# Moving half of the memory projections of a two-layer block from the opening to the border between the layers

## The chip, the cores and the metric

The kernel runs on one core of one Trainium2 chip. A core has a matrix engine (TensorE, "PE"), a vector engine (DVE), a scalar engine (ACT), GpSimd (POOL) and a queue for transfers on SyncE (SP). Each engine executes its own list of instructions in order; semaphores order them among each other. The metric is the device time of one execution in microseconds (us), lower is better.

## What is computed

Two blocks follow each other on the same 512 x 1024 activations; the change touches the first. It has two layers, and both attend to one memory of 256 rows, with keys and values of their own:

```python
def mem_cross_attention(q_mem, mem_n, w_kv):
    kv = mem_n @ w_kv                     # 256 x 1024 @ 1024 x 1024
    km, vm = split_cols(kv, [MEM_W, MEM_W])
    ...
    s = einsum('bshd,bmhd->bhsm', q, km) / sqrt(HEAD_DIM)
    return einsum('bhsm,bmhd->bshd', softmax(s), vm)

def first_block(x, mem, ...):
    mem_n = rmsnorm(mem, mem_norm_g)
    for i in range(2):
        h = rmsnorm(x, norm_g[i])
        # i == 0: forgetting attention, i == 1: retention
        proj = h @ w_in[i]
        memo = mem_cross_attention(q_mem, mem_n, w_mem_kv[i])
        o = concat([main, memo]) * silu(z)
        x = x + o @ w_out[i]
    return rmsnorm(x, final_norm_g)
```

`mem_n` is the same for both layers, so the keys and values of layer 2 can be made at any time before its memory attention.

## The kernel before

All matrices are float32. Every operand is split into a high half (rounded, `wh`, `HH`, `MH`) and a low half (the rest, `wl`, `HL`, `ML`), and each product is three matmuls: high by high, high by low, low by high. Activations lie transposed: X is 8 tiles of 128 features x 512 tokens, the memory MX is 8 tiles of 128 x 256.

**Weights** arrive in a planned order (`weight_plan`, line 95) as blocks of 512 KB, 128 x 1024. SP loads them into five buffers `raw` (`load_raw`, 278). `split_next` (321) makes a block's halves in one of three buffers: ACT copies raw to `wh`, then POOL subtracts to give `wl`, after which the raw buffer is loaded anew. `take` (342) hands the next block, a **slot**, to the matmuls; when it hands out slot u, it has put the splits up to slot u + 2 on ACT's and POOL's lists, and the split of u + 2 waits until the matmuls of slot u - 1 have released its buffer. Some blocks ("ada", 303) are no slots: DVE multiplies them with a vector, for the second block of the model.

**A unit** is two slots, 1024 x 256 weights: `unit_f` (393, out features x tokens, two banks) and `unit_t` (398, tokens x out features) each have 2 x 24 matmuls, on bank 0 and 1 unless told otherwise. The banks' owner before must have been read out (`bank.free`).

**The opening** (line 495 on). SP issues the loads: parameters, a raw block, the memory in two halves, a raw block, constants, a raw block, X in one piece, raw blocks. ACT and DVE make MH and ML, then the squares of the memory (`add_square`, 433: ACT squares into one of two buffers T, DVE adds up in ACC). A loop of eight units follows, `i` = 0 to 7: four for layer 1 and four for layer 2, two of keys (km) and two of values (vm) each, all on banks 0 and 1. The memory's 1/rms is applied when a unit's result is stored; `mem_rstd` (527) makes it: matmuls with ones sum over features, ACT does Ln, Exp (row form RM), Ln, Exp (column form). It stands between the halves of unit 0. Beside units 1 and 2 X is squared, `acc_rstd` (462) after unit 3 makes R, the 1/rms of X, and beside units 4 to 7 `normed` (467) makes two tiles of HH and HL each: DVE multiplies X by the gain and R into a T buffer, ACT copies to HH, and POOL (two of three tiles) or DVE subtracts to HL and so frees T. Then a single slot gives the forget gate (`slot_128`), tile by tile, and `layer_mem` (695) makes the queries and gates of the memory heads.

**The end of layer 1.** `project_out` (670) has 16 slots in four groups n of four q, all on banks 0 and 1. `steps` at (n, q) are put out right behind that slot's matmuls. After the fourth slot of a group DVE adds the banks to X tiles 2n and 2n+1, which frees the banks, and `add_square` follows each addition:

```python
            for j in range(2):
                t = 2 * n + j
                m = tt(X[:, t, :], X[:, t, :], bank[j].ap, ALU.add, ...)
                bank[j].free = [m]
                ... add_square(X[:, t, :], ...)
```

**The border.** After it `next_h` (849) makes R and all eight tiles of HH and HL, and `layer_mem(1, ...)` begins with a unit that needs them.

Of the kernel before, what the change touches and what calls it, by code (L numbers as in the profile page):

```python
# [8 lines left out]
ALU = mybir.AluOpType  # L9
ACT = mybir.ActivationFunctionType  # L10
# [84 lines left out]
def weight_plan():  # L95

    plan = []

    def pair(w, k0, k1, cols):
        for k in range(k0, k1, 4):  # L100
            plan.append(("w", w, k, cols))

    def ada(i):
        plan.append(("ada", i // 8, i % 8, None))

    left = list(range(47, -1, -1))
    for i in range(8):
        pair("kv%d" % (i // 4), 0, 8, (256 * (i % 4),))
    plan.append(("f", "fox", 0, None))
    for cols in [4620, 5132 + 1536, 4876, 5132 + 1792]:  # L110
        pair("fox", 0, 8, (cols,))
        ada(left.pop())
        ada(left.pop())
    for p in range(6):
        for cols in (1536 + 256 * p, 256 * p, 3072 + 256 * p, 5132 + 256 * p):
            pair("fox", 0, 8, (cols,))
            ada(left.pop())
            if p < 2:
                ada(left.pop())
    for n in range(4):  # L120
        for k in (12, 0, 4, 8):
            pair("out0", k, k + 4, (256 * n,))
            if left:
                ada(left.pop())
    for cols in [3072, 3584 + 1536, 3328, 3584 + 1792]:
        pair("ret", 0, 8, (cols,))
    for p in range(6):
        for cols in ((128 * p, 768 + 128 * p), (1536 + 256 * p,), (3584 + 256 * p,)):
            pair("ret", 0, 8, cols)
    for n in range(4):  # L130
        for k in (12, 0, 4, 8):
            pair("out1", k, k + 4, (256 * n,))
    for cols in (512, 1024, 768, 1280, 0, 256, 2560, 1536):
        pair("in2", 0, 8, (cols,))
    plan.append(("g", "in2", 0, None))
    for cols in (1792, 2048, 2304, 2816):
        pair("in2", 0, 8, (cols,))
    for n in range(4):
        pair("out2", 0, 8, (256 * n,))

    def up(g):
        for n in range(4):
# [19 lines left out]
def build(nc, a, out, stack):  # L162
# [10 lines left out]

    pe, dve, act, pool, sp = (Line(count("s_" + n)) for n in ("pe", "dve", "act", "pool", "sp"))
    s_raw = [count("s_raw%d" % i) for i in range(NRAW)]
    s_x, s_par = count("s_x"), count("s_par")
    s_mem = [count("s_mem%d" % i) for i in range(2)]
    s_sw = [count("s_sw%d" % i) for i in range(2)]
    s_d = [count("s_d%d" % i) for i in range(2)]
# [141 lines left out]
    def split_next():  # L321
        i = st["split"]
        if i >= len(plan):
            return False
        st["split"] += 1
        s, m = i % NRAW, landed[i]
        kind = plan[i][0]
        if kind == "ada":
            ada(plan[i][1], plan[i][2], s, m)
            load_raw()  # L330
            return split_next()
        u = st["nsplit"]
        st["nsplit"] += 1
        q = u % NW
        m1 = copy(wh[:, q, :], raw[:, s, :], after=[m, *w_free[q]])
        m2 = pool.do(G.tensor_tensor, wl[:, q, :], raw[:, s, :], wh[:, q, :].bitcast(F32), ALU.subtract, after=[m1])
        raw_free[s] = [m2]
        ready[u] = m2
        load_raw()
        return True  # L340
# [126 lines left out]
    def normed(src, g, rm, n, xh, xl, after, bias=None, ks=range(8), before=None, scale=None):  # L467
# [21 lines left out]
        if low:  # L489
# [2 lines left out]
        return ms  # L492


    MX = at("MX", [128, 8, 256], 148)
    MH, ML = at("MH", [128, 8, 256], 124, F32R), at("ML", [128, 8, 256], 132, F32R)
    maskf = at("maskf", [128, 128], 183.5)
    RM = at("RM", [128, 256], C0 + 8)
    m_par = sp.dma(SP.dma_start, par[:, :], a["par"], s_par)
    load_raw()  # L500
    m_mem = [sp.dma(SP.dma_start, MX[:, 4 * i:4 * i + 4, :], a["memT"][:, 4 * i:4 * i + 4, :], s_mem[i])
             for i in range(2)]
    load_raw()
    m_cst = sp.dma(SP.dma_start, ident[:, :], a["cst"][:, 0:128], s_c[0])
    m_cst = sp.dma(SP.dma_start, ones[:, :], a["cst"][:, 128:256], s_c[0])
    m_cst = sp.dma(SP.dma_start, maskf[:, :], a["cst"][:, 256:384], s_c[0])
    M["cst"], M["par"] = m_cst, m_par
    load_raw()
    m_x = sp.dma(SP.dma_start, X[:, :, :], a["xT"], s_x)
    for _ in range(NRAW - 3):  # L510
        load_raw()
    m = dve.do(V.memset, eps[:, 0:1], 1e-6)
    M["eps"] = dve.do(V.memset, one, 1.0)
    mem_h = Tiles()
    split_next()
    for k in range(8):
        m = copy_scaled(MH[:, k, :], MX[:, k, :], P("gm", k), [m_mem[k // 4], m_par])
        mem_h.high.append(m)
        mem_h.append(stt(ML[:, k, :], MX[:, k, :], P("gm", k), MH[:, k, :].bitcast(F32), ALU.mult, ALU.subtract,
                         after=[m]))  # L520
        if k == 3:
            split_next()
    for k in range(8):
        add_square(MX[:, k, :], 256, k == 0, [m_mem[k // 4]])
    rcol = small["tq"]

    def mem_rstd():

        e, m = rstd(ACC[:, 0:256], [M["acc"]], 256, 1024, RM[:, :], [], bank[6])
        for t in range(2):  # L530
            e = mm(bank[7].ap[:, t:t + 1], ACC[:, 128 * t:128 * t + 128], ones[:, 0:1], t == 0, t == 1,
                   after=[*bank[7].free], mark=(t == 1))
        m2 = afn(rcol[:, 0:2], bank[7].ap[:, 0:2], ACT.Ln, after=[e], scale=1.0 / 1024, bias=eps[:, 0:1])
        bank[7].free = [m2]
        M["acc free"] = [e]
        return m, afn(rcol[:, 0:2], rcol[:, 0:2], ACT.Exp, after=[m2], scale=-0.5)

    M["kv"], x_h = [], Tiles()
    for i in range(8):
        l, j = i // 4, i % 4  # L540
        if j < 2:
            for kh in range(2):
                features(MH, ML, range(4 * kh, 4 * kh + 4), 256, kh == 0, kh == 1, mem_h, bank[0:2])
                if i + kh == 0:
                    m_rm, m_rc = mem_rstd()
            e0 = tt(km[l][:, 2 * j, :], bank[0].ap[:, 0:256], RM[:, :], ALU.mult, after=[bank[0].done, m_rm])
            e1 = tt(km[l][:, 2 * j + 1, :], bank[1].ap[:, 0:256], RM[:, :], ALU.mult, after=[bank[1].done])
            bank[0].free, bank[1].free = [e0], [e1]
        else:
            unit_t(MH, ML, 2, mem_h)  # L550
            for t in range(2):
                e1 = copy_scaled(vm[l][:, t, 256 * (j - 2):256 * (j - 2) + 256], bank[0].ap[:, 256 * t:256 * t + 256],
                                 rcol[:, t:t + 1], [bank[0].done, m_rc])
            bank[0].free = [e1]
        M["kv"].append(e1)
        if i == 0:
            vcopy(identb[:, :], ident[:, :], after=[m_cst])
            M["bf"] = vcopy(maskb[:, :], maskf[:, :])
            for n, d in (("c", small["sc"]), ("cc", small["scc"])):
                m = afn(d[:, :], P(n, 0, 8), ACT.Tanh, after=[m_par], scale=0.5)  # L560
                m = ts(d[:, :], d[:, :], 1.0, 0.5, ALU.add, ALU.mult, after=[m])
                silu_c.append(tt(d[:, :], d[:, :], P(n, 0, 8), ALU.mult, after=[m, m_par]))
        if i in (1, 2):
            for k in range(4 * i - 4, 4 * i):
                add_square(X[:, k, :], T, k == 0, [m_x])
        if i == 3:
            rm = acc_rstd(T)
        if 3 < i:
            ks = range(2 * i - 8, 2 * i - 6)
            part = normed(X, lambda k: P("g0", k), rm, T, HH, HL, [m_par], ks=ks)  # L570
            x_h += part
            x_h.high += part.high
# [97 lines left out]
    def project_out(l, steps):  # L670

        for n in range(4):
# [146 lines left out]
    for p in range(6):  # L819
# [904 lines left out]
```

How the kernel before makes its waits and increments, by code:

```python
    def replay(self, eng):  # L72
        for w in self.work:
            if w[0] is None:
                eng.wait_ge(w[1], w[2])
            else:
                i = w[0](*w[1], **w[2])
                if w[3] is not None:
                    i.then_inc(w[3], w[4])
```

## Time and profile before

| | us |
|---|---|
| three runs, median (lowest to highest) | 1754.67 (1751.62 to 1755.99) |
| the profiled execution, first to last instruction | 1755.0 |
| PE busy | 1668.5 (95%) |
| DVE, ACT, POOL busy | 779.3, 670.3, 712.4 |
| chain that ended last: PE, DVE, ACT, POOL | 81%, 10%, 4%, 2% |
| POOL wl, 246 times | 2497 ns each |
| ACT wh, 246 times | 1054 ns each |

The rows of the next section come from a profile of one execution. A timeline row is: start (us), duration (us), engine, line, operation, what it writes and reads, count. Where an engine sat idle before it, the brackets give for how long and what ended that. PEclk is the granted clock of PE as a share of 2.4 GHz.

### The profile page before, as it was taken

How to read it: one execution, taken by the hardware profiler on the slowest of the kernel's cores; microseconds unless marked ns; L12 is line 12 of the kernel's file. 1: busy time of each engine (PE TensorE's matmuls, PEld its weight loads, DVE VectorE, ACT ScalarE, POOL GpSimd, SP SyncE). 2: the span in 40 equal slices, each digit the busy share in tenths (PEclk: the TensorE clock that was granted, in tenths of full speed). 3: DMA queues.
4: the chain of work that ended last, by engine and by line, in shares of the span. 5: the costliest groups of instructions: out<-in, count | busy, mean ns of one | idle time of the engine just before them, and what ended most of it. 6: DMA issues, size and time to landing. Idle time of an engine off the chain costs nothing.

```text
span 1755.0 us, 19876 instructions
## 1 busy us (share of the span) xinstructions
PE 1668.5 (95%) x8208; PEld 1364.0 (78%) x8208; DVE 779.3 (44%) x1083; ACT 670.3 (38%) x966; POOL 712.4 (41%) x333
## 2 busy tenths in 40 slices
PE   5898999999999899999999999989989899999997
PEld 5776888888878677888887767778977688888885
DVE  5588775564653333443432646563262421111113
ACT  6543333333322342444444453225633443232322
POOL 4744334433334343333333324342412265454542
PEclk9999999999999999999999999999999999999999
DMA  6434343324244223223323222112201133222221
GB/s 228 133 114 159 136 147 136 138 97 150 89 144 151 72 73 114 82 92 102 96 91 112 73 108 72 48 72 75 73 1 36 61 112 100 99 100 96 96 84 48
DMA packets 51953, 175.98 MB, mean 100 GB/s; under 512 B 6284, under 2 KB 6924, under 8 KB 51352
## 3 DMA queue, kind: packets, MB, share of 16 engines
q1 hardware_dynamic: 51864, 174.73, 28.9%
q8 instruction: 64, 1.05, 0.2%
q14 instruction: 25, 0.20, 0.0%
HBM read 169.44 MB, written 2.12 MB: 98 GB/s over the span
## 4 chain that ended last, share of the span: by engine, by line
PE 81%; DVE 10%; ACT 4%; POOL 2%; issue 2%; DMA 1%; SPq 0%; DVEq 0%; ACTq 0%; POOLq 0%
PE banks L77 81%; DVE T L77 2%; DVE ada L77 2%; ACT L77 1%; DVE TM L77 1%; POOL wl L77 1%; DVE Sc L77 1%; DVE X L77 1%; ACT R L77 1%; DVE ACC L77 0%; ACT Sc L77 0%; ACT wh L77 0%; DVE HL L77 0%; DVE Y L77 0%; DMA raw<-wst_dram 0%
## 5 line engine op out<-in xcount | busy, mean ns | idle before, releaser
L77 POOL TENSOR_TENSOR wl<-raw,wh 128x1024 fp32r<-128x1024 f32 x246 | 612.3, 2497 | 674.4 <-ACT wh L77 674.4
L77 PE MATMUL banks<-HH,wh 128*128 128x512 f32 x1040 | 416.9, 401 | 13.9 <-ACT HH L77 9.1
L77 PE MATMUL banks<-HL,wh 128*128 128x512 f32 x1040 | 408.0, 392 | 1.0 <-DVE HL L77 0.4
L77 PE MATMUL banks<-HH,wl 128*128 128x512 f32 x1040 | 407.2, 392 | 0.0
L77 ACT ACTIVATE wh<-raw 128x1024 fp32r<-128x1024 f32 x246 | 257.6, 1054 | 380.6 <-PE banks L77 354.5
L77 PEld LDWEIGHTS banks<-HH,wh 128*128 128x128 f32 x1040 | 196.9, 189 | 61.6 <-issue 15.5
L77 PEld LDWEIGHTS banks<-HL,wh 128*128 128x128 f32 x1040 | 196.1, 189 | 46.1 <-DVE HL L77 3.1
L77 PEld LDWEIGHTS banks<-HH,wl 128*128 128x128 f32 x1040 | 197.0, 189 | 42.0 <-issue 2.6
L77 PE MATMUL banks<-wh,HH 128*128 128x256 f32 x448 | 128.7, 287 | 2.0 <-ACT QX L77 2.0
L77 PE MATMUL banks<-wh,HL 128*128 128x256 f32 x448 | 127.4, 284 | 0.0
L77 PE MATMUL banks<-wl,HH 128*128 128x256 f32 x448 | 127.4, 284 | 0.0
L77 PE MATMUL banks<-OH,wh 128*128 128x512 f32 x256 | 104.4, 408 | 3.0 <-DVE X L77 2.2
L77 DVE SCALAR_TENSOR_TENSOR X<-banks,mod,X 128x512 f32<-128x512 f32 x40 | 30.0, 751 | 163.3 <-PE banks L77 163.3
L77 PE MATMUL banks<-OL,wh 128*128 128x512 f32 x256 | 100.0, 391 | 0.0
L77 PE MATMUL banks<-OH,wl 128*128 128x512 f32 x256 | 100.0, 391 | 0.0
L77 PE MATMUL banks<-FHI,wh 128*128 128x512 f32 x256 | 99.6, 389 | 0.0
L77 PE MATMUL banks<-FHI,wl 128*128 128x512 f32 x256 | 99.6, 389 | 0.0
L77 PE MATMUL banks<-FLO,wh 128*128 128x512 f32 x256 | 99.6, 389 | 0.0
L77 POOL TENSOR_TENSOR OL<-T,OH 128x512 fp32r<-128x512 f32 x22 | 29.2, 1328 | 171.0 <-ACT OH L77 171.0
L77 ACT ACTIVATE T<-banks 128x512 f32<-128x512 f32 x78 | 46.5, 596 | 122.3 <-PE banks L77 121.3
L77 PEld LDWEIGHTS banks<-wh,HH 128*128 128x128 f32 x448 | 86.6, 193 | 3.6 <-issue 2.8
L77 ACT ACT_TABLE_LOAD x69 | 88.5, 1283 | 2.0 <-PEq L1715 0.7
(285 smaller groups left out, 2578.1 us busy)
## 6 DMA issues: line engine op xcount, KB each, us to landing
raw<-wst_dram SPq DMA_DIRECT2D x294, 512.0 KB, 3.3
CB<-sums_dram SPq DMA_DIRECT2D x12, 256.0 KB, 3.0
D<-dec_dram SPq DMA_DIRECT2D x12, 256.0 KB, 2.6
X<-xT_dram SPq DMA_DIRECT2D x1, 2048.0 KB, 10.7
out_dram<-X SPq DMA_DIRECT2D x8, 256.0 KB
QS<-QX SPq DMA_DIRECT2D x24, 64.0 KB, 2.6
KSw<-KX SPq DMA_DIRECT2D x24, 64.0 KB, 2.0
MX<-memT_dram SPq DMA_DIRECT2D x2, 512.0 KB, 6.0
```

The source lines that it names most:

```text
L77: i = w[0](*w[1], **w[2])
```

## The change

- The plan has four pairs of kv blocks in the opening and four, for layer 2, behind `out0`.
- In the opening the memory's squares come ahead of the first unit, into ACC2. Units rotate over the bank pairs (0, 1), (2, 3), (4, 5), (0, 1). `mem_rstd` is put out after unit 1, R of X after unit 2, and HH and HL are made in two groups of four tiles around unit 3. X comes in two loads. Slot 0's low half is made by DVE.
- In `project_out(0)` the memory is loaded again (into HH's place), split into MH and ML and squared in two steps, and its 1/rms is made at (2, 3).
- At the border unit 0 of layer 2 runs first, then R of X is put out, then HH and HL in groups of 2, 3 and 3 tiles with a unit behind each.

```diff
-    for i in range(8):
-        pair("kv%d" % (i // 4), 0, 8, (256 * (i % 4),))
+    for i in range(4):
+        pair("kv0", 0, 8, (256 * i,))
...
+    for i in range(4):
+        pair("kv1", 0, 8, (256 * i,))
     for cols in [3072, 3584 + 1536, 3328, 3584 + 1792]:
         pair("ret", 0, 8, (cols,))
...
-        m2 = pool.do(G.tensor_tensor, wl[:, q, :], raw[:, s, :], wh[:, q, :].bitcast(F32), ALU.subtract, after=[m1])
+        if u == 0:
+            m2 = tt(wl[:, q, :], raw[:, s, :], wh[:, q, :].bitcast(F32), ALU.subtract, after=[m1])
+        else:
+            m2 = pool.do(G.tensor_tensor, wl[:, q, :], raw[:, s, :], wh[:, q, :].bitcast(F32), ALU.subtract, after=[m1])
...
+    def load_mem(l, after=()):
+        memory[l]["at"] = [sp.dma(SP.dma_start, memory[l]["MX"][:, 4 * i:4 * i + 4, :], a["memT"][:, 4 * i:4 * i + 4, :],
+                                  s_mem[i], after=after) for i in range(2)]
+
+    def mem_half(l, k, after=()):
+
+        d = memory[l]
+        h = d.setdefault("h", Tiles())
+        m = copy_scaled(d["MH"][:, k, :], d["MX"][:, k, :], P("gm", k), [d["at"][k // 4], m_par, *after])
+        h.high.append(m)
+        h.append(stt(d["ML"][:, k, :], d["MX"][:, k, :], P("gm", k), d["MH"][:, k, :].bitcast(F32), ALU.mult, ALU.subtract,
+                     after=[m]))
...
+    def mem_rstd(l):
+
+        d = memory[l]
+        last = M.pop("last", None)
+        e, m = rstd(ACC2[:, 0:256], [M["acc2"]], 256, 1024, d["RM"][:, :], [M["v read"]] if l else [], bank[6])
+        for t in range(2):
+            e = mm(bank[7].ap[:, t:t + 1], ACC2[:, 128 * t:128 * t + 128], ones[:, 0:1], t == 0, t == 1,
+                   after=[*bank[7].free], mark=(t == 1))
+        m2 = afn(rcol[:, 0:2], bank[7].ap[:, 0:2], ACT.Ln, after=[e], scale=1.0 / 1024, bias=eps[:, 0:1])
...
+    pairs = [bank[0:2], bank[2:4], bank[4:6], bank[0:2]]
...
+    mem_squares(0, range(8))
+    kv_matmuls(0, 0, pairs[0])
+    x_squares(range(0, 3))
+    kv_matmuls(0, 1, pairs[1])
+    mem_rstd(0)
+    for j in range(2):
+        kv_store(0, j, pairs[j])
+    vcopy(identb[:, :], ident[:, :], after=[m_cst])
+    M["bf"] = vcopy(maskb[:, :], maskf[:, :])
+    x_squares(range(3, 8))
+    kv_matmuls(0, 2, pairs[2])
+    rm = acc_rstd(T)
+    kv_store(0, 2, pairs[2])
+    for ks in (range(0, 4), range(4, 8)):
+        part = normed(X, lambda k: P("g0", k), rm, T, HH, HL, [m_par], ks=ks)
+        x_h += part
+        x_h.high += part.high
+        if ks[0] == 0:
+            kv_matmuls(0, 3, pairs[3])
+    kv_store(0, 3, pairs[3])
...
-    project_out(0, {(0, 0): [lambda: fox_turn(11)], (0, 1): [lambda: fox_attend(11)]})
+    h_read = M["v read"]
+
+    def mem_again(ks):
+        for k in ks:
+            mem_half(1, k, [M["v read"], M["z read"], M["pt read"]])
+        mem_squares(1, ks)
+
+    project_out(0, {(0, 0): [lambda: load_mem(1, [h_read]), lambda: fox_turn(11)], (0, 1): [lambda: fox_attend(11)],
+                    (1, 0): [lambda: mem_again(range(0, 4))], (2, 0): [lambda: mem_again(range(4, 8))],
+                    (2, 3): [lambda: mem_rstd(1)]})
...
-    M["pe"] = bank[1].done
-    hs = next_h(lambda k: P("g1", k))
+    out0_done = bank[1].done
+
+    pairs = [bank[2:4], bank[4:6], bank[0:2], bank[2:4]]
+    hs = Tiles()
+    kv_matmuls(1, 0, pairs[0])
+    rm = acc_rstd(T)
+    kv_store(1, 0, pairs[0])
+    for j, ks in ((1, range(0, 2)), (2, range(2, 5)), (3, range(5, 8))):
+        part = normed(X, lambda k: P("g1", k), rm, T, HH, HL, [M["x", 7], out0_done, memory[1]["h"][-1]], ks=ks)
+        hs += part
+        hs.high += part.high
+        kv_matmuls(1, j, pairs[j])
+        kv_store(1, j, pairs[j])
+    M["pe"] = pairs[3][0].done
```

`kv_matmuls` is the unit's matmuls as before, `kv_store` the multiplication by 1/rms into km (DVE) or vm (ACT), `mem_squares` the squares of MX.

## Rows read from the trace of the kernel before

**Rows 1.** The page's table of engines: busy us, share of the span, instructions.
```profile
PE 1668.5 (95%) x8208; PEld 1364.0 (78%) x8208; DVE 779.3 (44%) x1083; ACT 670.3 (38%) x966; POOL 712.4 (41%) x333
```

**Rows 2.** Timeline of PE in the opening: matmuls with idle time before them.
```profile
8.66 0.58 PE L77 MATMUL banks<-MH,wh 128*128 128x256 f32 x1 [8.66 <-POOL wl L77]
...
18.74 1.22 PE L77 MATMUL banks<-ACC,ones 128*128 128x256 f32 x2 [5.14 <-DVE ACC L77]
...
71.47 0.58 PE L77 MATMUL banks<-wh,MH 128*128 128x256 f32 x1 [2.53 <-POOL wl L77]
...
81.22 0.47 PE L77 MATMUL banks<-HH,wh 128*128 128x512 f32 x1 [1.02 <-ACT vm L77]
...
88.50 0.50 PE L77 MATMUL banks<-HH,wh 128*128 128x512 f32 x1 [1.56 <-DVE R L77]
```

**Rows 3.** Windows: length, PE, PEld, DVE, ACT, POOL busy (instructions), PEclk, DMA, GB/s.
```profile
20.50:23.00 2.50, 2.50 (x13) 2.50 (x14) 0.00 (x0) 2.45 (x4) 0.97 (x1) 0.50 0.21 57
62.90:68.90 6.00, 5.97 (x48) 5.81 (x48) 4.80 (x3) 3.17 (x4) 6.00 (x4) 1.00 0.55 175
70.90:77.60 6.70, 6.13 (x28) 6.13 (x29) 6.67 (x4) 2.12 (x3) 6.70 (x4) 0.50 0.48 159
602.30:606.70 4.40, 4.12 (x8) 2.21 (x8) 3.06 (x3) 1.79 (x3) 2.50 (x2) 0.50 0.00 0
```

**Rows 4.** Timeline of PE in the projection's beginning and at the border.
```profile
507.72 0.69 PE L77 MATMUL banks<-ident,Sc 128*128 128x128 f32 x2 [3.01 <-DVE Sc L77]
...
602.31 0.76 PE L77 MATMUL banks<-HH,wh 128*128 128x512 f32 x1 [4.36 <-ACT HH L77]
...
617.70 0.59 PE L77 MATMUL banks<-km,Qt 128*128 128x256 f32 x2
```

**Rows 5.** Timeline of POOL in the opening: low halves of slots 0 and 2.
```profile
6.26 2.34 POOL L77 TENSOR_TENSOR wl<-raw,wh 128x1024 fp32r<-128x1024 f32 x1 [5.82 <-ACT wh L77]
...
19.11 2.36 POOL L77 TENSOR_TENSOR wl<-raw,wh 128x1024 fp32r<-128x1024 f32 x1 [5.80 <-ACT wh L77]
```

**Rows 6.** Timelines of POOL and DVE: tile normalisation beside wl, and alone.
```profile
53.08 5.19 POOL L77 TENSOR_TENSOR wl<-raw,wh 128x1024 fp32r<-128x1024 f32 x2 [3.32 <-ACT wh L77]
...
54.61 4.20 DVE L77 SCALAR_TENSOR_TENSOR T<-X,par,R 128x512 f32<-128x512 f32 x2
...
600.75 1.41 DVE L77 SCALAR_TENSOR_TENSOR T<-X,par,R 128x512 f32<-128x512 f32 x2 [4.64 <-ACT R L77]
```

**Rows 7.** Timeline of ACT: the chains of the memory's and of X's 1/rms.
```profile
19.05 1.28 ACT L77 ACT_TABLE_LOAD   x1
20.34 0.47 ACT L77 ACTIVATE RM<-banks,eps 128x256 f32<-128x256 f32 x1
...
25.44 0.20 ACT L77 ACTIVATE tq<-tq 128x2 f32<-128x2 f32 x1
...
48.12 1.28 ACT L77 ACT_TABLE_LOAD   x1
...
51.42 0.63 ACT L77 ACTIVATE R<-R 128x512 f32<-128x512 f32 x1
```

**Rows 8.** Timelines of DVE and ACT around the end of slot (2, 3).
```profile
570.94 0.69 DVE L77 TENSOR_TENSOR X<-X,banks 128x512 f32<-128x512 f32 x1
...
573.66 0.69 DVE L77 TENSOR_TENSOR X<-X,banks 128x512 f32<-128x512 f32 x1 [0.64 <-PE banks L77]
...
571.66 0.64 ACT L77 ACTIVATE T<-X 128x512 f32<-128x512 f32 x1 [3.21 <-DVE X L77]
```

**Rows 9.** Timeline of POOL: the last low half at the border.
```profile
613.28 1.29 POOL L77 TENSOR_TENSOR HL<-T,HH 128x512 fp32r<-128x512 f32 x1 [1.96 <-DVE HL L77]
```

**Rows 10.** The page's list of DMA issues: KB each, us to landing.
```profile
X<-xT_dram SPq DMA_DIRECT2D x1, 2048.0 KB, 10.7
```

**Rows 11.** Timeline of ACT in the output projection: one slot's high half.
```profile
545.62 1.06 ACT L77 ACTIVATE wh<-raw 128x1024 fp32r<-128x1024 f32 x1 [4.38 <-PE banks L77]
```

**Rows 12.** Groups by form, 0 to 100 us: busy, mean ns, idle before.
```profile
L77 DVE SCALAR_TENSOR_TENSOR T<-X,par,R 128x512 f32<-128x512 f32 x8 | 17.5, 2227 | 1.2 <-POOL HL L77 1.2
```

More of the change, by code:

```diff
@@ L175, in build @@
     s_raw = [count("s_raw%d" % i) for i in range(NRAW)]
-    s_x, s_par = count("s_x"), count("s_par")
+    s_x, s_par = [count("s_x%d" % i) for i in range(2)], count("s_par")
     s_mem = [count("s_mem%d" % i) for i in range(2)]
@@ L492, in normed @@
         return ms
-    MX = at("MX", [128, 8, 256], 148)
-    MH, ML = at("MH", [128, 8, 256], 124, F32R), at("ML", [128, 8, 256], 132, F32R)
     maskf = at("maskf", [128, 128], 183.5)
-    RM = at("RM", [128, 256], C0 + 8)
+    rcol = small["tq"]
+    memory = [dict(MX=at("MX0", [128, 8, 256], 148), MH=at("MH0", [128, 8, 256], 124, F32R),
+                   ML=at("ML0", [128, 8, 256], 132, F32R), RM=at("RM0", [128, 256], C0 + 8)),
+              dict(MX=at("MX1", [128, 8, 256], 60), MH=at("MH1", [128, 8, 256], C0, F32R),
+                   ML=at("ML1", [128, 8, 256], C0 + 8, F32R), RM=at("RM1", [128, 256], C0 + 16))]
@@ new lines, in mem_squares @@
+    def mem_squares(l, ks):
+        for k in ks:
+            add_square(memory[l]["MX"][:, k, :], 256, k == 0, [memory[l]["at"][k // 4]], ACC2, name="acc2")
+    def mem_rstd(l):
[6 more added lines that the diff above has]
+        m2 = afn(rcol[:, 0:2], bank[7].ap[:, 0:2], ACT.Ln, after=[e], scale=1.0 / 1024, bias=eps[:, 0:1])
+        bank[7].free = [m2]
+        M["acc2 free"] = [e]
+        d["rm"], d["rc"] = m, afn(rcol[:, 0:2], rcol[:, 0:2], ACT.Exp, after=[m2], scale=-0.5)
+        if last:
+            M["last"] = last
@@ new lines, in kv_matmuls, with kv_store @@
+    def kv_matmuls(l, j, banks):
+        d = memory[l]
+        if j < 2:
+            for kh in range(2):
+                features(d["MH"], d["ML"], range(4 * kh, 4 * kh + 4), 256, kh == 0, kh == 1, d["h"], banks)
+        else:
+            unit_t(d["MH"], d["ML"], 2, d["h"], banks)
+    def kv_store(l, j, banks):
+        d = memory[l]
+        if j < 2:
+            e0 = tt(km[l][:, 2 * j, :], banks[0].ap[:, 0:256], d["RM"][:, :], ALU.mult, after=[banks[0].done, d["rm"]])
+            e1 = tt(km[l][:, 2 * j + 1, :], banks[1].ap[:, 0:256], d["RM"][:, :], ALU.mult, after=[banks[1].done])
+            banks[0].free, banks[1].free = [e0], [e1]
+        else:
+            for t in range(2):
+                e1 = copy_scaled(vm[l][:, t, 256 * (j - 2):256 * (j - 2) + 256], banks[0].ap[:, 256 * t:256 * t + 256],
+                                 rcol[:, t:t + 1], [banks[0].done, d["rc"]])
+            banks[0].free = [e1]
+        M["kv"].append(e1)
@@ L499, in build @@
     m_par = sp.dma(SP.dma_start, par[:, :], a["par"], s_par)
     load_raw()
-    m_mem = [sp.dma(SP.dma_start, MX[:, 4 * i:4 * i + 4, :], a["memT"][:, 4 * i:4 * i + 4, :], s_mem[i])
-             for i in range(2)]
+    load_mem(0)
     load_raw()
@@ L508, in build @@
     load_raw()
-    m_x = sp.dma(SP.dma_start, X[:, :, :], a["xT"], s_x)
+    m_x = [sp.dma(SP.dma_start, X[:, 4 * i:4 * i + 4, :], a["xT"][:, 4 * i:4 * i + 4, :], s_x[i]) for i in range(2)]
     for _ in range(NRAW - 3):
@@ L513, in build @@
     M["eps"] = dve.do(V.memset, one, 1.0)
-    mem_h = Tiles()
     split_next()
     for k in range(8):
[L517 to L520, printed above, removed]
+        mem_half(0, k)
         if k == 3:
             split_next()
-    for k in range(8):
-        add_square(MX[:, k, :], 256, k == 0, [m_mem[k // 4]])
@@ L525, in build @@
[L525 to L536, printed above, removed]
@@ L538, in build @@
-    M["kv"], x_h = [], Tiles()
[L539 to L572, printed above, removed]
@@ new lines, in build, with x_squares @@
+    M["kv"], x_h = [], Tiles()
+    pairs = [bank[0:2], bank[2:4], bank[4:6], bank[0:2]]
+    def x_squares(ks):
+        for k in ks:
+            if k == 7:
+                last_square(X[:, k, :], [m_x[1]])
+            else:
+                add_square(X[:, k, :], T, k == 0, [m_x[k // 4]])
+    mem_squares(0, range(8))
[6 more added lines that the diff above has]
+    vcopy(identb[:, :], ident[:, :], after=[m_cst])
@@ new lines, in build @@
+    M["bf"] = vcopy(maskb[:, :], maskf[:, :])
[10 more added lines that the diff above has]
+    kv_store(0, 3, pairs[3])
+    for n, d in (("c", small["sc"]), ("cc", small["scc"])):
+        m = afn(d[:, :], P(n, 0, 8), ACT.Tanh, after=[m_par], scale=0.5)
+        m = ts(d[:, :], d[:, :], 1.0, 0.5, ALU.add, ALU.mult, after=[m])
+        silu_c.append(tt(d[:, :], d[:, :], P(n, 0, 8), ALU.mult, after=[m, m_par]))
@@ L679, in project_out @@
                 t = 2 * n + j
-                m = tt(X[:, t, :], X[:, t, :], bank[j].ap, ALU.add, after=[bank[j].done, m_x])
+                m = tt(X[:, t, :], X[:, t, :], bank[j].ap, ALU.add, after=[bank[j].done, *m_x])
                 bank[j].free = [m]
@@ L844, in build @@
         fox_scores(2 * p + 1)
-    project_out(0, {(0, 0): [lambda: fox_turn(11)], (0, 1): [lambda: fox_attend(11)]})
-    M["R free"] = [M["v read"], *M["R free"]]
-    def next_h(g, bias=None, extra=()):
-        rm = acc_rstd(T)
-        return normed(X, g, rm, T, HH, HL, [M["x", 7], M["pe"], *extra], bias)
-    M["pe"] = bank[1].done
-    hs = next_h(lambda k: P("g1", k))
+    h_read = M["v read"]
+    def mem_again(ks):
+        for k in ks:
+            mem_half(1, k, [M["v read"], M["z read"], M["pt read"]])
[3 more added lines that the diff above has]
+                    (2, 3): [lambda: mem_rstd(1)]})
+    M["R free"] = [M["v read"], *M["R free"]]
+    out0_done = bank[1].done
[11 more added lines that the diff above has]
+    M["pe"] = pairs[3][0].done
     QA, QB, KR = at("QA", [128, T], C0), at("QB", [128, T], C0 + 2), at("KR", [128, T], C0 + 4)
```

## Prediction

> **What bounds the kernel now.** I read the page's engine table first: TensorE (PE) is busy for 95% of 1755.0 us [rows 1]. The change computes nothing less and nothing more (four units of 48 matmuls move from one place to another), so its worth can only lie in PE's idle time and in time at the lower clock, at the two places it touches. I then read PE's own timeline for the idle time ahead of each matmul, and the other engines' timelines for what ended it.
>
> In the opening PE starts at 8.66 us, when POOL has made the first low half, waits 5.14 us at 18.74 for the squares of the memory, and then loses 1 to 2.5 us at nearly every unit; ahead of the second, third and fourth unit of layer 2 it is a wait for POOL's wl (1.27, 1.41 and 2.53 us; the last is shown). The forget slot starts at 81.22 and the layer's first full unit at 88.50 [rows 2]. One unit of memory keys or values (2 slots, 48 matmuls) is 6.00 us between 62.90 and 68.90 with the granted clock at 1.00, of which 5.97 busy; started without a wait it is 48 x 0.12 = 5.7 us. At the clock's lower level (1.2 against 2.4 GHz; granted 0.50 in the stretches from 20.5, 70.9 and 602.3) a matmul of 256 columns takes 0.21 us [rows 3]. All 8 units are thus 46 us of the opening's 88.5; idle time is some 26 us.
>
> At the border PE waits 4.36 us for HH at 602.31 and reaches the first memory scores at 617.70: a unit of 10.9 us (48 x 0.227) has taken 15.4 [rows 4]. So the border loses about 4.4 + 4.5 = 9 us, the most that the moved units could hide.
>
> **The change, part by part.**
>
> *u == 0 on DVE.* POOL's first wl takes 2.34 us [rows 5]; on DVE, two operands of 1024 elements, it is about 1.4 us by two 512-element operations in 1.41 [rows 6]. PE starts 0.85 us earlier. Nothing comes of it: the third slot's wh still stands on ACT behind the eight squares of the memory, and its wl still runs at 19.11 for 2.36 us [rows 5]. Both of the first unit's slots are done by 16.5 now that the normalising matmuls are not between them, and PE then waits until 21.5 for the third slot.
>
> *Opening, four units in place of eight.* I chain it on. Idle for 5 us, PE comes back at the lower level: 24 x 0.21 = 5.1, to 26.6; the fourth slot, 24 x 0.12, to 29.5. Only then stand mem_rstd's matmuls (18.74 before) in PE's queue. Its ACT chain after the first table load is 20.34 to 25.64 = 5.3 us [rows 7]; the matmuls take 1.2, so it ends at 29.5 + 1.2 + 5.3 = 36.0. Behind it on ACT are x squares 3 to 7, five at about 0.75 (ACT 0.63, DVE 0.69 in turn [rows 8]), to 39.8, and two wh of 1.05, to 41.9. R's chain is 48.12 to 52.05 = 3.9 us [rows 7]: R at 45.8, 6.2 us earlier than before, though 22.9 us of matmuls are gone. The bank pairs in rotation take away waits of 2 us on km and vm stores, but PE then waits for ACT in their place.
>
> From R on, HH and HL of all eight tiles: at the border, with nothing between, 600.75 to 614.57 = 13.8 us [rows 6, 9]; here two weight splits stand in the middle. They add 2.1 us on ACT and about 2 us of collisions: beside POOL's wl (53.08, 5.19 us for two) DVE takes 4.20 us for the two T operations from 54.61 that take 1.41 alone [rows 6]. So HL is complete at 45.8 + 18 = 63.8 and the forget slot, which goes tile by tile, ends at 64.5 against 86.9 (81.22 and 24 x 0.227 with its start): **-22.4**. Its last half trickles over some 7 us, so PE begins the next unit at the lower level: +1.5 (0 to 3). Opening **-21**, between -25.5 (third slot at full clock, no collisions) and -18. Silu of c, the two CASTs and the extra X issue on SP lie beside this chain (X lands at 5.70 + 10.7 = 16.4 [rows 10], before its first square); if they did not, they would cost under 1 us.
>
> *mem_again in the output projection.* At steps (1,0) and (2,0) ACT gets 4 copies and 4 squares, at most 0.63 each (a tile twice as wide [rows 8]), 5 us, and DVE 8 operations. ACT is idle some 4 us of each 5.4-us slot there [rows 11] and a split has two slots of lead; X's additions come three slots later. Cost 0; if the cover were gone, some 2 us each. The memory's reload (1 MB on SP's queue, behind raw loads) has over 10 us until (1,0): 0.
>
> *mem_rstd(1) at step (2,3).* This is the step I find expensive. It is emitted after the slot's matmuls but ahead of the additions of X tiles 4 and 5. PE: its matmuls, 1.0 us at full clock (1.7 before at the lower one). ACT: Ln, load, Exp, load, Ln, load, Exp (its first table load runs ahead): 5.3 us. DVE's queue is X4 +=, ACC += square of X4, X5 +=, in order [rows 8]. The square of X4 now stands behind ACT's chain, so DVE's ACC waits, X5 += waits behind it, and that addition frees bank 1. With slot (2,3) ending at E = 573.6: chain over at E+6.0, square E+6.6, ACC E+7.3, X5 E+8.0. PE starts slot (3,0) at E+1.0, is through its first bank at E+3.7 and waits until E+8.0 for bank 1: 4.3 us. An idle time of 3.01 us at 507.72 was followed by a stretch at the lower level [rows 4]; I take 1.2 for that. Sum **+6.5** (4.5 to 8.5). The Trainium skill, ScalarE: Activation LUTs, section Table sets, says that one set holds both exp and ln, so that Ln then Exp need one load. By that rule three of the four loads, 3.8 us, would be gone and the wait would be 0.5. The rows show a load of 1.28 us before each of the four [rows 7], and the sum goes by them.
>
> *Border.* Let the projection's last slot end at 0 (595.3 before). The first unit's slots A and B run at once, 0 to 5.7, then R's matmuls, to 7.5. ACT has split C (2.4) and D (4.0), but is then in R's chain until 10.2, where before R was ready at 5.4; no split can be made meanwhile. C and D end at 13.2. HH of tiles 0 and 1, then wh E: 13.4, wl E: 15.9: PE waits 2.7. Next stand T2 to T4 on DVE, each behind one of POOL's wl E and F as in [rows 6], HL2 and HL3 on POOL, and T4 behind HL2's buffer: HH4 at 22.5, wh G 23.5, wl G 26.2. E and F end at 21.9: PE waits 4.2. Again for T5 to T7, wl G and H, HL5 and HL6: HH7 at 32.7, wl I at 36.4; H ends at 32.2: PE waits 4.2. The layer's first unit runs 36.4 to 47.3, and 49.3 with a stretch at the lower level; before it ended at 22.4. So **+27** (22 to 30). A check by rows: before, four units with two tiles each ran from 48.25 to 81.22, 33 us; here R comes 6.4 us later, part of which the two first units cover.
>
> **Sum.** -21 + 6.5 + 27 = +12.5 on the execution's 1755.0, whose median of runs is 1754.67: 1767. In words: each place's matmuls cancel (-22.9, +22.9); the opening stays bound by ACT's chains and keeps its idle time, and the border, meant to be covered, has more waits for wl than it had for HH, plus the bank-1 wait. The ends of the three terms, none of which pulls the others with it, leave 1758 to 1774.
>
> **Rivals.**
> *Faster: DVE and POOL do not hold each other up here, and splits keep ahead.* If the T operations take 0.7 and wl comes in time, the opening gives -25.5, and at the border the four units run in 22.9 + 1.8, the first full unit ends at 35.7: +13.3; with the bank wait +5: 1748. It decides if wl E and G are ready before D and F end. Against it: the three idle gaps of this kind before were ended by POOL wl, and eight T operations took 17.5 us there [rows 2, 12]. The Trainium skill, SBUF, section Who interferes with whom, has an exclusive lock for a VectorE operation with two SBUF inputs against a GpSimd one that reads SBUF; the trace agrees by the 4.20 against 1.41 us.
> *The bank-1 wait does not appear* (ACT takes the square in time, or loads overlap): 1767 - 5.5 = 1761; together with a milder border (22) it reaches 1756, within the bound of no change. For it speaks only that ACT is lightly loaded there; against it, the queues' order.
> *Worse: PE never warms up at the border.* Waits of 4 us every 10 us hold the lower level through G, H and the first unit, and the opening's units also run at it: +4 at each place, 1775.
>
> **How the numbers follow.** Forecast (1758 to 1774) 0.60; faster rival (1743 to 1753) 0.14; no bank wait, with or without a milder border (1754 to 1762) 0.16; worse (1774 to 1784) 0.10. 0.3% is about what a measurement can tell: bounds 1749.4 and 1759.9. Faster 0.12; within 0.23 (part of the first rival, half of the second, the forecast's low end); slower 0.65. The range 1750 to 1777 leaves out most of the faster rival and half of the worst.
>
> **What would show it.** PE idle before the third slot until about 21.5; the first full unit near 66 (not below 62); PE idle 3 to 5 us in the first slot of the projection's last quarter, ended by DVE X; three PE gaps ended by POOL wl between border and first full unit, which ends 27 us after where it did. Wrong if those gaps are under 1 us, or if R in the opening comes before 40 us.

## The result and the profile after

The changed kernel takes 1770.12 us (median; 1767.76 to 1771.81, 4 runs) beside 1753.14 us of the kernel before in the same runs: a ratio of 1.009 (95% interval 1.0068 to 1.0112), slower. The forecast was 1767 with a range of 1750 to 1777. The profiled execution spans 1769.2 us, 14.2 more than the 1755.0 of before. Of all executions in this document one stood far off in a slow state, at 5235.45 us (of g_before_rotate, below), and no ratio counts it (the median of 1751.68 given for that kernel does; without it it is 1750.34).

The page of the changed kernel, engines and costliest groups:

```profile
PE 1672.8 (95%) x8216; PEld 1369.6 (77%) x8216; DVE 785.0 (44%) x1099; ACT 682.0 (39%) x990; POOL 711.2 (40%) x332
...
L77 PE MATMUL banks<-HH,wh 128*128 128x512 f32 x1040 | 417.5, 401 | 20.8 <-ACT sc L77 11.4
...
L77 PE MATMUL banks<-OH,wh 128*128 128x512 f32 x256 | 106.4, 415 | 7.0 <-DVE X L77 6.2
```

PE is busy 4.3 us longer than before [rows 1], 0.3%. Two new waits show: 11.4 us put down to ACT sc, and 6.2 in the output projections of both layers put down to DVE X, where it was 2.2 before:

```profile
L77 PE MATMUL banks<-OH,wh 128*128 128x512 f32 x256 | 104.4, 408 | 3.0 <-DVE X L77 2.2
```

Where the time lies shows when both traces are cut at the same three instructions, the first product of queries and keys of the memory in layer 1, the addition of X tile 7 at the end of the projection, and layer 2's first such product:

| stage | before | after | difference |
|---|---|---|---|
| opening, to layer 1's first memory scores | 99.5 | 84.0 | -15.6 |
| layer 1, to the addition of X tile 7 | 495.9 | 502.8 | +6.9 |
| border, to layer 2's first memory scores | 22.3 | 47.1 | +24.8 |
| the rest | 1137.3 | 1135.4 | -1.9 |

PE's timeline in the opening of the changed kernel, matmuls with idle time before them (beside [rows 2]):

```profile
8.12 0.55 PE L77 MATMUL banks<-MH,wh 128*128 128x256 f32 x1 [8.12 <-ACT MH L77]
...
22.08 0.58 PE L77 MATMUL banks<-MH,wh 128*128 128x256 f32 x1 [4.86 <-POOL wl L77]
...
43.31 0.58 PE L77 MATMUL banks<-wh,MH 128*128 128x256 f32 x1 [0.82 <-POOL wl L77]
...
62.92 0.76 PE L77 MATMUL banks<-HH,wh 128*128 128x512 f32 x1 [11.42 <-ACT sc L77]
```

ACT's timeline in the same stretch:

```profile
36.17 0.20 ACT L77 ACTIVATE tq<-tq 128x2 f32<-128x2 f32 x1
...
45.08 0.63 ACT L77 ACTIVATE R<-R 128x512 f32<-128x512 f32 x1
...
60.76 1.29 ACT L77 ACTIVATE HH<-T 128x512 fp32r<-128x512 f32 x2 [2.26 <-DVE T L77]
61.96 0.82 ACT L77 ACTIVATE vm<-banks,tq 128x256 f32<-128x256 f32 x2
62.67 0.20 ACT L77 ACTIVATE sc<-par 128x8 f32<-128x8 f32 x1
```

The chain of the prediction stands here within 0.6 us: slot 2 starts at 22.1 (forecast 21.5), the memory's 1/rms is ready at 36.4 (36.0), R at 45.7 (45.8). But the forget slot starts only at 62.92, and layer 1's first full unit at 72.94, where "near 66" was forecast. The profile names ACT's sc; a cheap tanh of a parameter cannot be what a matmul of HH waits for. The instruction just ahead of it on ACT is the store of the opening's last unit (vm), over at 62.78, and that store frees bank 0, on which the forget slot begins. Until then PE had been idle 11.4 us.

Windows of the changed kernel over this wait and behind it (columns as in [rows 3]):

```profile
51.50:62.90 11.40, 0.01 (x1) 0.01 (x1) 9.42 (x6) 4.83 (x11) 9.13 (x6) 0.66 0.27 93
62.90:68.60 5.70, 5.68 (x13) 4.44 (x14) 0.93 (x4) 1.02 (x2) 2.87 (x2) 0.50 0.21 63
```

After 11.4 idle microseconds PE runs its next 13 matmuls of 512 columns at a granted clock of 0.50, 5.68 us where 0.227 each would make 3.0.

The end of slot (2,3) of the projection: timelines of ACT, DVE and PE (beside [rows 8]):

```profile
557.41 0.47 ACT L77 ACTIVATE RM<-banks,eps 128x256 f32<-128x256 f32 x1 [4.37 <-PE banks L77]
...
562.50 0.20 ACT L77 ACTIVATE tq<-tq 128x2 f32<-128x2 f32 x1
562.61 0.61 ACT L77 ACTIVATE T<-X 128x512 f32<-128x512 f32 x1
...
563.26 0.69 DVE L77 TENSOR_TENSOR ACC<-ACC,T 128x512 f32<-128x512 f32 x1 [8.31 <-ACT T L77]
563.87 0.68 DVE L77 TENSOR_TENSOR X<-X,banks 128x512 f32<-128x512 f32 x1
...
564.60 0.80 PE L77 MATMUL banks<-OH,wh 128*128 128x512 f32 x1 [4.03 <-DVE X L77]
```

Each link follows the one above it: the chain of the 1/rms ends at 562.7, then come the square of X tile 4, its sum, the addition of tile 5, and PE, idle 4.03 us.

The border: PE's waits, and DVE and POOL beside the second of them:

```profile
602.38 0.39 PE L77 MATMUL banks<-wh,MH 128*128 128x256 f32 x1 [2.46 <-POOL wl L77]
...
612.95 0.58 PE L77 MATMUL banks<-wh,MH 128*128 128x256 f32 x1 [4.55 <-POOL wl L77]
...
622.81 0.50 PE L77 MATMUL banks<-HH,wh 128*128 128x512 f32 x1 [1.50 <-POOL wl L77]
...
599.98 5.16 POOL L77 TENSOR_TENSOR wl<-raw,wh 128x1024 fp32r<-128x1024 f32 x2 [6.13 <-ACT wh L77]
...
600.30 5.39 DVE L77 SCALAR_TENSOR_TENSOR T<-X,par,R 128x512 f32<-128x512 f32 x2
...
605.10 3.00 POOL L77 TENSOR_TENSOR HL<-T,HH 128x512 fp32r<-128x512 f32 x2
606.88 1.77 DVE L77 SCALAR_TENSOR_TENSOR T<-X,par,R 128x512 f32<-128x512 f32 x1 [1.19 <-POOL HL L77]
```

Two T operations (DVE's multiplications of X into a T buffer) last 5.39 us beside POOL's two wl of 5.16, in place of 1.41 [rows 6]. The third waits for HL to free a T buffer, and the split for the next unit stands behind it on ACT.

### The profile page after: what moved, and what is told of

Same layout as the page of the kernel before. It is cut to its first block, busy times and chain, and to the rows that moved or that the text cites. A ratio compares the mean times of both kernels' runs of the same rounds, so it can differ in the third digit from the quotient of the medians.

```text
span 1769.2 us, 19937 instructions
## 1 busy us (share of the span) xinstructions
PE 1672.8 (95%) x8216; PEld 1369.6 (77%) x8216; DVE 785.0 (44%) x1099; ACT 682.0 (39%) x990; POOL 711.2 (40%) x332
## 4 chain that ended last, share of the span: by engine, by line
PE 80%; DVE 10%; ACT 5%; issue 2%; POOL 2%; DMA 1%; SPq 0%; DVEq 0%; ACTq 0%; POOLq 0%
PE banks L77 80%; DVE T L77 2%; DVE ada L77 2%; ACT L77 1%; POOL wl L77 1%; DVE TM L77 1%; DVE Sc L77 1%; ACT wh L77 1%; DVE ACC L77 1%; DVE X L77 1%; ACT R L77 1%; ACT Sc L77 0%; DMA raw<-wst_dram 0%; DVE Y L77 0%; ACT T L77 0%
## 5 line engine op out<-in xcount | busy, mean ns | idle before, releaser
L77 PE MATMUL banks<-HH,wh 128*128 128x512 f32 x1040 | 417.5, 401 | 20.8 <-ACT sc L77 11.4
L77 PEld LDWEIGHTS banks<-HH,wl 128*128 128x128 f32 x1040 | 197.2, 190 | 42.5 <-issue 2.6
```

Source lines behind the costliest of these rows:

```text
L77: i = w[0](*w[1], **w[2])
```

## The experiments

Each kernel was run beside the kernel before, and ratios are to that; a to e are the changed kernel with one edit each. The changed kernel's own ratio is 1.009. The interval of every one of a, b, d and e overlaps with that of the changed kernel, so what a single edit did is read from the traces. Stage times are from each kernel's trace, cut as in the table above:

| kernel | opening | layer 1 | border | rest | ratio (95% interval) |
|---|---|---|---|---|---|
| before | 99.5 | 495.9 | 22.3 | 1137.3 | 1 |
| changed | 84.0 | 502.8 | 47.1 | 1135.4 | 1.009 (1.0068 to 1.0112) |
| a_rstd22 | 83.1 | 495.7 | 47.1 | 1135.4 | 1.0058 (1.0036 to 1.0080) |
| b_store_early | 78.8 | 501.7 | 47.1 | 1135.4 | 1.0067 (1.0045 to 1.0088) |
| c_low0_pool | 82.8 | 502.2 | 47.1 | 1135.2 | one run |
| d_r_bank | 80.3 | 498.0 | 43.5 | 1135.9 | 1.0056 (1.0037 to 1.0075) |
| e_groups2 | 82.3 | 502.2 | 42.5 | 1133.3 | 1.0062 (1.0044 to 1.0081) |
| f_all | 78.1 | 495.9 | 40.3 | 1136.5 | 0.9955 (0.9939 to 0.9970) |
| g_before_rotate | 96.1 | 495.8 | 22.3 | 1137.2 | 0.9985 (0.9973 to 0.9997) |
| h_before_rot_bank | 91.9 | 494.1 | 20.4 | 1132.7 | 0.9940 (0.9924 to 0.9956) |

Four spreads are to be kept in mind. An opening repeats to 1 or 2 us (84.0, 83.1, 82.3, 82.8 in four kernels whose opening is the same or all but the same). A wait of PE between 150 and 175 us is 0.35 to 4.2 us long in kernels with the same code there, and is the main cause of the spread in the layer 1 column; it was not studied. At the start of the projection PE works for a while at the lower clock in seven traces (a granted clock of 0.81 over 8.8 us) and not in c, d and e (1.00), which makes their projection 1.8 us shorter. And the rest, whose code is the same everywhere, runs from 1132.7 to 1137.3. The traces of a, b, d, e and h are of the fastest of each kernel's executions, that of f of its slowest.

**The wait in the projection.** The 1/rms of the memory is put out one slot earlier.

```diff
-                    (2, 3): [lambda: mem_rstd(1)]})
+                    (2, 2): [lambda: mem_rstd(1)]})
```

> The changed kernel with the memory's 1/rms put out one slot earlier, at (2,2). Theory (the addition of X tile 5 stood behind the square of tile 4, and that behind ACT's chain of 5.3 us with its table loads): from the end of slot (2,2) the chain ends at +6.0, the square of tile 4 at +6.6, ACC at +7.3, X5 at +8.0, and bank 1 is needed at +9.2, so PE's gap of 4.03 us in slot (3,0) and the stretch at the lower clock behind it are gone: 5 to 6 us less than the changed kernel, near 1764.5. Rival (the gap belongs to the chain wherever it stands): a gap of 3 to 4 us stays one slot earlier or in the same place, and the time stays at 1770.

The median is 1764.11 us beside 1754.42. That is 6.0 less than the changed kernel, as expected, and in part by luck: in the trace the projection is only 3.9 us shorter, and the rest of its 8.0 us less lies mainly in the unstudied wait (1.70 in place of 3.81) and in the opening. The wait for X is gone, but the theory had missed another: the transposes that sum up an ada vector follow at the next slot and use banks 6 and 7, which this 1/rms holds. PE's timeline, then ACT's:

```profile
550.86 0.66 PE L77 MATMUL banks<-ident,ada 128*128 128x128 f32 x4 [2.65 <-ACT tq L77]
...
550.55 0.26 ACT L77 ACTIVATE tq<-banks,eps 128x2 f32<-128x2 f32 x1
```

ACT's second Ln reads bank 7 until 550.8; then PE goes on. A wait of 4.03 us with a stretch at the lower clock has become one of 2.65 without (granted clock 1.00 from 547.5 to 558.8). From the wait at the projection's start to the addition of tile 7 it is 87.7 us before, 95.7 changed, 91.8 here and 88.6 in f_all, where the chain stands at (2,1) and PE has no wait over 0.3 us: the wait cost 7.1, the matmuls of the chain 0.9.

**The wait for bank 0 in the opening.** The store of the last unit is put out right behind the unit.

```diff
         if ks[0] == 0:
             kv_matmuls(0, 3, pairs[3])
-    kv_store(0, 3, pairs[3])
+            kv_store(0, 3, pairs[3])
```

> The changed kernel with the store of the opening's last unit (ACT, which frees bank 0) put out right behind that unit instead of behind the second four tiles. Theory (in the opening PE's gap of 11.4 us ahead of the forget slot is bank 0 waiting for a store that stands behind HH of tile 7 on ACT): the forget slot starts at 55 to 57 when its wl is there, goes tile by tile, ends near 64.5 instead of 71.4, and the time is 6 to 7 us less, near 1763.5. Rival (the gap is the tiles' own lateness, as the prediction had it): the slot still ends within 1.5 us of 71.4 and nothing is gained.

The median is 1765.68 us beside 1754.42, 4.4 less than the changed kernel where 6 to 7 were expected. PE's timeline in the opening:

```profile
54.00 0.80 PE L77 MATMUL banks<-HH,wh 128*128 128x512 f32 x1 [5.77 <-POOL wl L77]
61.66 0.50 PE L77 MATMUL banks<-HH,wh 128*128 128x512 f32 x1 [0.85 <-DVE HL L77]
62.95 0.50 PE L77 MATMUL banks<-HH,wh 128*128 128x512 f32 x1 [0.33 <-POOL HL L77]
66.24 0.80 PE L77 MATMUL banks<-HH,wh 128*128 128x512 f32 x1 [2.32 <-DVE R L77]
```

Now the forget slot starts at 54.0 with its wl, takes the tiles as they come, and the next unit starts at 66.24 and not at 72.94. The opening is 5.2 us shorter than the changed kernel's, 3.5 to 4.4 shorter than those of a, c and e. So the store's place on ACT was the cause, and not the tiles. It was not the whole of the 11.4 us: PE still waits 5.77 here, for the slot's own wl, which in the changed kernel was there at 54.5; from then on only the store held its first matmul.

**Slot 0's low half.** POOL makes it again.

```diff
-        if u == 0:
+        if False:
             m2 = tt(wl[:, q, :], raw[:, s, :], wh[:, q, :].bitcast(F32), ALU.subtract, after=[m1])
```

> The changed kernel with slot 0's low half on POOL again. Theory (PE waits for slot 2's wl anyway): PE starts 0.5 to 0.9 us later, slot 2 still starts at about 22.1, the time is unchanged. Rival (the start carries through): everything behind is 0.5 to 0.9 us later.

One run gives 1769.49 us. PE starts at 8.81 us (8.12 in the changed kernel), slot 2 at 22.19 (22.08). The early start is lost before the third slot; this part of the change is worth nothing here, as far as one run tells.

**Does DVE wait for POOL?** R goes to PSUM bank 7 for both layers, so that the tile operations have one operand in SBUF. R itself is still computed in the same way.

```diff
+        if to is not None:
+            return e, afn(to, dst, ACT.Exp, after=[m, *to_free], scale=-0.5)
         return e, afn(dst, dst, ACT.Exp, after=[m], scale=-0.5)
...
-    rm = acc_rstd(T)
+    rm = acc_rstd(T, to=bank[7].ap, to_free=bank[7].free)
...
-        part = normed(X, lambda k: P("g1", k), rm, T, HH, HL, [M["x", 7], out0_done, memory[1]["h"][-1]], ks=ks)
+        part = normed(X, lambda k: P("g1", k), rm, T, HH, HL, [M["x", 7], out0_done, memory[1]["h"][-1]], ks=ks, scale=bank[7].ap)
+        bank[7].free = M["R free"]
```

> The changed kernel with R, the 1/rms of X, left by ACT in PSUM bank 7 for both layers, so that the tile normalisation on DVE has one SBUF operand, and not two. Lock theory alone (DVE's T operations wait out POOL's wl, and that sets the pace of the splits): T operations fall from 2.2 to 2.8 us to 0.75 beside wl, the border's gaps of 4.6 and 1.5 us go, 7 us or more less. Theory with POOL's own queue (HL of a tile stands behind two wl and frees the T buffer late, lock or not): T operations fall to 0.75, but wl G comes only 1.8 us and wl I 3 us earlier; 3 to 4 us less in all, near 1766.5. No contention at all: T operations stay as they are, no gain.

The median is 1763.26 us beside 1754.42, 6.9 less than the changed kernel where 3 to 4 were expected. Groups by form at the border, of the changed kernel (590 to 625 us) and of this one (585 to 625):

```profile
L77 DVE SCALAR_TENSOR_TENSOR T<-X,par,R 128x512 f32<-128x512 f32 x8 | 13.8, 1757 | 8.7 <-POOL HL L77 4.7 <-ACT R L77 4.0
```

```profile
L77 DVE SCALAR_TENSOR_TENSOR T<-X,par,banks 128x512 f32<-128x512 f32 x8 | 5.7, 743 | 13.1 <-POOL HL L77 9.2 <-ACT banks L77 3.9
```

PE's waits there:

```profile
593.97 0.39 PE L77 MATMUL banks<-wh,MH 128*128 128x256 f32 x1 [2.44 <-POOL wl L77]
...
602.40 0.39 PE L77 MATMUL banks<-wh,MH 128*128 128x256 f32 x1 [2.41 <-POOL wl L77]
...
610.83 0.50 PE L77 MATMUL banks<-HH,wh 128*128 128x512 f32 x1 [0.92 <-POOL wl L77]
```

An operation takes 0.743 us on average, and all eight take 0.74 or 0.75 whatever POOL does, where the average was 1.757: with R in SBUF they shut each other out, with R in PSUM they do not. But of the 8.1 us that DVE gained, 4.5 turned into waiting for POOL's HL to free a T buffer (4.7 to 9.2 us), and the border is 3.6 us shorter: the second theory, with POOL's own queue. The opening is 2.0 to 3.6 us shorter too, more than that theory had; the layer 1 column owes its 4.8 us mainly to the unstudied wait (0.35 us here) and to the missing stretch at the lower clock. The first wait (2.44) has not moved, nor does it in e and f: the prediction lays it to R's chain on ACT, ahead of all tiles, and nothing here speaks against that, but no run took that chain away. The opening's wait for bank 0 is still there too (11.96 us, to 60.69).

**The groups at the border.**

```diff
-    for j, ks in ((1, range(0, 2)), (2, range(2, 5)), (3, range(5, 8))):
+    for j, ks in ((1, range(0, 2)), (2, range(2, 4)), (3, range(4, 6)), (4, range(6, 8))):
...
-        kv_matmuls(1, j, pairs[j])
-        kv_store(1, j, pairs[j])
+        if j < 4:
+            kv_matmuls(1, j, pairs[j])
+            kv_store(1, j, pairs[j])
```

> The changed kernel with the border's tiles in groups of 2, 2, 2 and the last 2 behind the fourth unit, instead of 2, 3, 3. Theory (the third tile of a group waits for a T buffer that POOL frees only after two wl, and the next weight split stands behind it on ACT): the high half of slot G comes some 2.5 us earlier, the gap of 4.55 us ahead of it falls to about 2, the later gap of 1.5 to under 1, the stretch at the lower clock shrinks; 3 to 5 us less than the changed kernel's 1770, near 1766. Rival (the wait only moves on): tiles 6 and 7 then stand behind two splits, the first full unit waits for HH and HL of these tiles, and no more than 1 us is won.

The median is 1767.37 us, the ratio 1.0062: 2.8 less than the changed kernel, a little under the 3 to 5 expected. The border takes 42.5 us in place of 47.1. PE's second wait:

```profile
608.72 0.39 PE L77 MATMUL banks<-wh,MH 128*128 128x256 f32 x1 [2.52 <-POOL wl L77]
```

2.52 in place of 4.55, nothing over 0.3 us behind it, and the first full unit does not wait for tiles 6 and 7. The third tile of a group was one cause.

**Rotation alone.** The kernel before, its eight units on three bank pairs in turn.

```diff
         l, j = i // 4, i % 4
+        bk = bank[2 * (i % 3):2 * (i % 3) + 2]
...
-                features(MH, ML, range(4 * kh, 4 * kh + 4), 256, kh == 0, kh == 1, mem_h, bank[0:2])
+                features(MH, ML, range(4 * kh, 4 * kh + 4), 256, kh == 0, kh == 1, mem_h, bk)
...
-            unit_t(MH, ML, 2, mem_h)
+            unit_t(MH, ML, 2, mem_h, bk)
...
```

The stores read `bk` in the same way.

> The kernel before, with its eight units in the opening over the bank pairs (0,1), (2,3), (4,5) in turn and nothing else. If the waits for km and vm stores (1.99, 1.02, 0.16 and 1.02 us) are all that holds those units, up to 4 us less than before; if the weight splits are next, as the changed kernel's opening suggests, 1 to 2 us of it come back as waits for wl, and 1 to 3 us are won, within what can be told from none.

The median is 1751.68 us beside 1754.42, the opening 3.4 us shorter. Of the parts of the change that were run by themselves it is the one that pays, though by little: the interval ends at 0.9997. The waits on stores became waits on wl, as PE's timeline shows for the fourth and the eighth unit:

```profile
39.80 0.39 PE L77 MATMUL banks<-wh,MH 128*128 128x256 f32 x1 [1.71 <-POOL wl L77]
...
70.06 0.38 PE L77 MATMUL banks<-wh,MH 128*128 128x256 f32 x1 [2.51 <-POOL wl L77]
```

**The repairs together.** The kernel f_all is the changed kernel with the edits of b, d and e and with `mem_rstd(1)` at (2,1).

> The changed kernel with four repairs together: the memory's 1/rms at (2,1), where neither X's additions nor the reductions of the ada sums (which use the same two banks) follow closely, the opening's last store moved up, R in PSUM bank 7, groups of 2 tiles. If each is worth alone what it was (about 6, 4.4, 6.9 and, by expectation, 4 us) and the two that act on the opening's last stretch do not add fully, 1749 to 1754: level with the kernel before, 1754.4. If one common bound stands behind them (ACT's list in the opening, POOL's in the border), 1755 to 1760.

The median is 1747.31 us beside 1755.54, 0.45% faster than the kernel before: a little better than forecast. PE's waits at the border are 2.44, 1.19 and 0.41 us. Even so the border costs 18.0 us more than before and the opening 21.4 less, and the 3 us between them are not yet what the move of 22.9 us of matmuls is worth, because rotation and R in PSUM help the opening without it, as the next kernel shows.

**The units left where they were.** The kernel h_before_rot_bank is the kernel before with the edits of g and d (for both layers).

> The kernel before with the rotation over three bank pairs and R in PSUM bank 7 for both layers; layer 2's memory units stay in the opening. Theory (the lock between DVE's two-operand operations and POOL's wl cost the units beside the tiles 1 to 2.5 us each, whichever place they stand in): T operations fall from 2.2 to 0.75 us, the three gaps before the last units (0.87, 1.41, 2.51 us after rotation) fall by half or more with the stretch at the lower clock, 3 to 6 us on top of rotation's 2.7: 1746 to 1749, faster than both kernels. Rival (POOL's 2.4 us per wl and 1.3 per HL alone bound those units): gaps stay, 1751.

The median is 1745.15 us beside 1755.54, 0.6% faster; the lowest of all, without moving anything. Its interval and that of f_all overlap, so that which of the two is faster is not settled. Both have rotation and R in PSUM, and they differ in the move (with its repairs): in the traces f_all's opening is 13.9 us shorter than this kernel's and its border 19.9 longer. So no gain from the move itself is shown, even with nothing new in its way; the traces speak for a loss. Groups by form, 40 to 90 us (beside [rows 12]), and PE's waits ahead of the last units:

```profile
L77 DVE SCALAR_TENSOR_TENSOR T<-X,par,banks 128x512 f32<-128x512 f32 x8 | 5.8, 743 | 2.4 <-POOL HL L77 2.4
```

```profile
54.26 0.39 PE L77 MATMUL banks<-MH,wh 128*128 128x256 f32 x1 [0.84 <-POOL wl L77]
...
67.12 0.38 PE L77 MATMUL banks<-wh,MH 128*128 128x256 f32 x1 [1.09 <-POOL wl L77]
```

The waits of 0.87, 1.42 and 2.51 us of g have become 0.84, none over 0.3 and 1.09. The opening is 4.2 us shorter than with rotation alone. At the border it is 1.9 us shorter: the eight T operations take 0.747 us on average and not 1.005, HL of the tiles comes sooner, and from the first matmul of the full unit to the memory scores PE needs 13.5 us and not 15.4. The rest is 4.5 us shorter than in g, which is no more than that stage varies by in kernels that differ elsewhere.

## Why the prediction was right, and where it was off

**The whole.** +12.5 was forecast on the profiled execution, +14.2 came: -15.6 opening, -1.1 in layer 1 up to the projection's first wait (which is 1.96 us and no longer 3.01 [rows 4]), +8.0 from there to the addition of X tile 7, +24.8 at the border, -1.9 in the rest. The sign, the size and the places hold. That the sum is off by only 1.7 us is luck in part: the errors are +5.4 in the opening, +1.5 in the projection, -2.2 at the border, and -3.0 in stages that the forecast left alone and whose spread is as large.

**Opening, forecast -21, measured -15.6.** This is the term that was mis-sized. Up to R the steps named stand within 0.6 us, and HL was complete at 63.4 (63.8). The step that failed is "the forget slot goes tile by tile": I had named what each tile waits for, but not what the slot's first matmul waits for, bank 0, whose store stood behind HH of tile 7. In b, where the slot does go tile by tile, the next unit starts 22.3 us earlier than before (88.50 to 66.24; 22.4 was forecast) and then takes 12.5 us in place of 11.0 with a stretch at the lower clock (granted 0.72 in its first 5.8 us; +1.5 was forecast): 20.8 us in all. That it fits to the tenth is within an opening's own spread. In the changed kernel PE had 24 matmuls left from 62.9 on, 5.7 us of them at the lower clock.

**Low half of slot 0, forecast nothing:** c shows nothing.

**The projection, forecast +6.5, measured +8.0.** The wait was 4.03 (4.3), the chain on ACT 5.3 us as forecast, with a table load of 1.28 us ahead of each of its four steps and the first of them run in advance, and the chain's matmuls 0.9 (1.0). (The rows print two of the loads before; the trace has all four.) What was small is the loss by the clock: about 3 us, not 1.2, since PE came back at the lower level (first row below). `mem_again` and the reload were forecast at nothing. In f_all the projection with both in it is 0.9 us longer than before, and that is the chain's matmuls. The rival without this wait fell. Run a removed the wait for X, and the projection became 3.9 us shorter, f_all 7.1 us.

**Border, forecast +27, measured +24.8.** Of the three waits, 2.7, 4.2 and 4.2 were forecast, 2.46, 4.55 and 1.50 came. The third is short because PE worked at the lower level in the unit before it (second row: 23 matmuls that end there took some 2 us longer than at 0.12 each) and came late itself: the clock's loss lay where a wait would have been, and not in the first full unit, where I had put it (it took 11.0 us, at 1.00). Windows of the changed kernel:

```profile
564.60:570.20 5.60, 5.60 (x13) 4.49 (x14) 0.69 (x1) 1.56 (x2) 2.37 (x1) 0.50 0.10 23
611.40:618.00 6.60, 5.05 (x23) 5.05 (x24) 3.09 (x2) 1.67 (x4) 6.60 (x4) 0.51 0.41 141
```

**The faster rival** (DVE and POOL beside each other without loss) fell for the changed kernel: 5.39 us for two T operations. Runs d and h show that the mechanism it denied is real, and also what it is worth: taking it away at the border gave 3.6 us, not the 7 or more that d's first theory gave if it alone set the pace.

## What to carry to other kernels

When work is moved to another place, list for its first instruction everything that it waits for, the output buffer too, and look where on the releasing engine's list that release stands: a store of 0.8 us held the matrix engine from 54.5 to 62.9, and moving it up shortened the opening by some 4 to 5 us. Putting a chain with several waits of its own ahead of short operations that free a buffer makes the buffer wait for the chain. One slot earlier the chain met a third user of its banks and cost 2.65 us; two slots earlier it cost only its own 0.9 us of matmuls. And before moving work under a stall, see whether the engines that feed it have room there: the four units needed 8 weight splits on the same ACT and POOL that had to make the tiles, so what they covered came back as waits for weights, while two small edits gave as much at the old place as with the move.

## What the runs showed of the hardware

A DVE operation with two tensor operands in SBUF and POOL's subtraction exclude each other. With R in SBUF a T operation of the changed kernel's border took 0.75 us with POOL idle (1.42 for two that overlap a little, from 596.87), 1.77 beside an HL and 2.7 beside a wl (5.39 for two), 1.757 on average; with R in PSUM all eight took 0.74 or 0.75. So the PSUM operand costs the operation itself nothing. The Trainium skill, SBUF — State Buffer, section Who interferes with whom, states the exclusion; the trace agrees.

The clock's loss need not be a loss of time. The changed kernel's border had 6.6 us at a granted clock of 0.51 and then a wait of 1.50 us, where 4.2 had been worked out for full clock. I read this as slow matmuls that only shorten a wait for a split that comes when it comes; no run changed the clock alone.
